# 768 features of the experts' second weights copied into 3 KB rows and gathered for the second 128 tokens, with the feature groups taken in turn

## The reference, cut to what matters

```
u = jnp.take(peer_u, expert, axis=0)
act = jax.nn.gelu(jnp.einsum('chkd,cd->chk', u, zc))
v = jnp.take(peer_v, expert, axis=0)
w = (gate * act.astype(jnp.float32)).astype(zc.dtype)
return jnp.einsum('chk,chkd->cd', w, v).astype(zc.dtype)
```

## Time and profile before

| | before |
|---|---|
| median of 3 runs | 3041.22 us |
| lowest, highest run | 3038.93, 3041.25 us |
| span of the profiled execution | 3039.3 us |
| TensorE busy | 3026.3 us of the span |
| VectorE, ScalarE, GpSimd busy | 2088.4, 1564.2, 1106.6 us |
| DMA, mean over the span | 221 GB/s |
| read and written | 627.88 MB, 39.99 MB |

### The profile page before, as it was taken

The page is one execution under the profiler, slowest core; times in us unless marked ns, Lnnn a source line. Parts: engine busy times, 40 slices in busy tenths (PEclk is TensorE's granted clock), DMA queues, the critical chain, the costliest instruction groups (busy, mean ns, idle before and its releaser), DMA issues.

```text
span 3039.3 us, 42704 instructions
## 1 busy us (share of the span) xinstructions
PE 3026.3 (100%) x16292; PEld 2605.3 (86%) x16292; DVE 2088.4 (69%) x3053; ACT 1564.2 (51%) x2160; POOL 1106.6 (36%) x856
## 2 busy tenths in 40 slices
PE   9999999999999999999999999999999999999999
PEld 7888888888888888888888888888888888888887
DVE  8957986555655656666667699998766856545554
ACT  7654554544544544444445656666566534444443
POOL 0023368888876377787771300000422000000000
PEclk9999999999999999999999999999999999999999
DMA  7567877988888899999997655555565566666664
GB/s 257 169 206 261 321 210 198 242 213 215 214 214 278 287 283 286 284 286 288 291 287 203 193 183 173 174 179 187 188 193 175 188 170 210 189 206 194 193 193 148
DMA packets 398365, 670.73 MB, mean 221 GB/s; under 512 B 68048, under 2 KB 293584, under 8 KB 394960
## 3 DMA queue, kind: packets, MB, share of 16 engines
q1 hardware_dynamic: 306144, 574.70, 61.2%
q10 hardware_dynamic: 42864, 76.28, 7.2%
q0 software_dynamic: 49152, 17.01, 4.5%
HBM read 627.88 MB, written 39.99 MB: 220 GB/s over the span
## 4 chain that ended last, share of the span: by engine, by line
PE 92%; DVE 3%; issue 2%; ACT 1%; DMA 1%; POOL 1%; SPq 0%; ACTq 0%; POOLq 0%; DVEq 0%
PE G L571 40%; PE G L575 20%; PE G L628 3%; PE G L626 3%; PE G L627 3%; PE M L626 3%; PE M L627 3%; PE M L628 3%; PE M L653 2%; PE G L653 2%; PE M L654 2%; PE G L655 2%; PE G L654 2%; PE M L655 2%; DVE lo L1364 1%
## 5 line engine op out<-in xcount | busy, mean ns | idle before, releaser
L571 PE MATMUL G<-ZA,hi 128*128 128x512 f32 x5098 | 1765.2, 395 | 4.4 <-DVE lo L1364 2.3
L1364 DVE TENSOR_TENSOR lo<-raw,hi 128x1024 fp32r<-128x1024 f32 x1088 | 1336.8, 1242 | 568.2 <-ACT hi L953 565.6
L953 ACT ACTIVATE hi<-raw 128x1024 fp32r<-128x1024 f32 x1088 | 1130.1, 1055 | 620.8 <-DMA raw<-in_pv 334.4
L575 PE MATMUL G<-ZA,lo 128*128 128x256 f32 x5114 | 1389.2, 278 | 0.0
L571 PEld LDWEIGHTS G<-ZA,hi 128*128 128x128 f32 x5098 | 943.2, 188 | 210.8 <-DVE lo L1364 2.8
L575 PEld LDWEIGHTS G<-ZA,lo 128*128 128x128 f32 x5114 | 960.7, 188 | 16.6
L2075 POOL DMA_INDIRECT g_scratch<-sel,IDX x256 | 418.6, 1635 | 112.9 <-issue 81.4
L960 ACT ACTIVATE tA<-G 128x256 f32<-128x256 f32 x367 | 139.4, 380 | 549.0 <-PE G L575 546.0
L1370 DVE TENSOR_TENSOR tS<-G,tA 128x256 f32<-128x256 f32 x336 | 141.2, 421 | 310.1 <-ACT tA L960 307.0
L2092 POOL DMA_INDIRECT vrow<-in_pv,IXV x192 | 259.2, 1350 | 109.3 <-issue 51.2
L626 PE MATMUL G<-hi,ZB 128*128 128x512 f32 x512 | 199.4, 389 | 0.0
(11 more groups left out here) (374 smaller groups left out, 2860.8 us busy)
## 6 DMA issues: line engine op xcount, KB each, us to landing
raw<-in_pu SPq DMA_DIRECT2D x256, 512.0 KB, 4.5
raw<-in_pv SPq DMA_DIRECT2D x256, 512.0 KB, 6.1
raw<-in_w_in SPq DMA_DIRECT2D x192, 512.0 KB, 3.5
raw<-in_w_up SPq DMA_DIRECT2D x128, 512.0 KB, 4.2
raw<-in_w_down SPq DMA_DIRECT2D x128, 512.0 KB, 5.0
raw<-in_w_out SPq DMA_DIRECT2D x32, 512.0 KB, 3.5
raw<-in_wq SPq DMA_DIRECT2D x32, 512.0 KB, 5.1
g_scratch<-zero ACTq DMA_DIRECT2D x16, 1024.0 KB, 6.9
```

The costliest lines, as they stand in the source:

```text
L571: pe.matmul(G[:, 0:512], w, Z[:, k, :], start=first, stop=False, skip_group_check=True)
L575: m = pe.matmul(G[:, 0:256], lo[POS[u][p] % NRAW][:, k % 8, :], weights(u, p)[1][:, k, 0:256], start=False, stop=last, skip_group_check=True)
L953: act.activation(hi[w][:, :, :], raw[r][:, :].rearrange("p (k n) -> p k n", k=8), ACT.Copy).then_inc(s_hi, 1)
L1364: dve.tensor_tensor(lo[r][:, :, :], raw[r][:, :].rearrange("p (k n) -> p k n", k=8), hi[w][:, :, :].bitcast(F32), ALU.subtract).then_inc(s ...
```

## The change

The stage v works with 768 gathered features instead of 256, for the second 128 tokens, and the rows come from a copy in DRAM.

- 96 DMAs on ScalarE's queue (`widen`) copy the last 768 features of all experts from `peer_v` into `v_wide`, DRAM to DRAM, 512 KB each, in pieces of 512 bytes that land 3 KB apart. 30 are issued in units 4 to 39, 66 in units 66 to 163.
- Each pick is then one indirect DMA of a 3 KB row for each of 128 tokens. The early pieces, their spill and their return go. GpSimd issues 128 gathers and 128 reads of activations, at 5/2 a unit, in blocks of 2 picks with a ring of 5 blocks.
- Matmuls of the second token half: group 2 has 256 columns instead of 512, group 3 has none instead of 256.
- In chunks 0 to 6 the units go through the four feature groups in turn (`expert_part`); the last chunk keeps its order. Loads and splits of gates are spread over the chunk to fit.
- `vacc` is three times as long as before and lies over the ring of `tS` and `tA`.
- `g_scratch` and `h_scratch` are laid out with one contiguous row of 33 x 1024 elements (132 KB) per partition.

```diff
-WIDE = 256
+WIDE = 768
+FROM_Q = 16 - WIDE // 128
-BLOCK = 8
+BLOCK = 2
-RING = 3
+RING = 5
+COPY_AT = {u: n for n, u in enumerate([u for u in range(4, 40) if u % 6] + list(range(66, 165, 3)) + list(range(67, 166, 3)))}
+PITCH = 33 * 1024
+def expert_part(i, c):
+    return divmod(i, 4) if c == KEPT - 1 else divmod(i, 4)[::-1]
+def last_use(c, n):
+    return VB[c] + (12 + n // 2 if c == KEPT - 1 else 4 * (n // 2) + 3), n % 2
 def gate_kept_at(u):
-    c, n = divmod(u - VB[0] + 10, 16)
-    return (c, n - 2) if 0 <= c < KEPT and n in range(2, 6) else None
+    if VB[0] - 8 <= u < VB[0] - 4:
+        return 0, u - VB[0] + 8
+    c, n = divmod(u - VB[0] - 2, 16)
+    return (c + 1, n // 4) if n % 4 == 0 and 0 <= c < KEPT - 1 else None
 def picks_by(u):
-    return max(0, min((FETCHED + BLOCK) * PIECES, (u - VB[0] + 1) * 3 // 1))
+    return max(0, min(2 * 128, (u - VB[0] + 1) * 5 // 2))
 DOTS_AT = {}
 for _b in range(PIECES):
-    _u = min(v for v in range(VB[0], F0) if picks_by(v) >= (FETCHED + BLOCK) * (_b + 1)) + 6
...
+    _u = min(v for v in range(VB[0], F0) if picks_by(v) >= 2 * BLOCK * (_b + 1)) + 4
+    DOTS_AT.setdefault(_u, []).extend(range(BLOCK * _b, BLOCK * _b + BLOCK))
                 for x in range(2):
                     for h, G in enumerate(VM[q]):
+                        e = min(512, max(0, 128 * (FROM_Q - 4 * q))) if h else 512
+                        if not e:
+                            continue
-                        e = EDGE if q == 3 and h else 512
-                        act.wait_ge(s_mm, done(VB[c] - 4 + n // 2, n % 2))
+                        act.wait_ge(s_mm, done(*last_use(c - 1, n)))
+            def widen(n):
+                q, a = divmod(n, 16)
+                src = ins["pv"][FROM_Q + q, a].rearrange("p (b f) -> (p b) f", f=128)
+                act.dma_start(vwide[1024 * a:1024 * a + 1024, 128 * q:128 * q + 128], src).then_inc(s_vw, 16)
                 if u == F0:
                     expert_out(3)
+                    act.wait_ge(s_ved, 4)
-                b, k = divmod(n, FETCHED + BLOCK)
-                if k < FETCHED:
+                b, k = divmod(n, 2 * BLOCK)
+                if k < BLOCK:
+                    if n == 0:
+                        pool.wait_ge(s_mm, done(VB[0] - 1))
+                        pool.wait_ge(s_ixa, 11)
+                        pool.wait_ge(s_vw, 16 * len(COPY_AT))
                     if k == 0:
+                        pool.wait_ge(s_vrow, ROW_BASE + 16 * BLOCK * b)
                         if b >= RING:
                             pool.wait_ge(s_dot, BLOCK * (b - RING + 1))
                     at = BLOCK * b + k
+                    pool.indirect_dma_start(vrow[:, slot_of(b), k, :], None, vwide,
+                                            bass.IndirectOffsetOnAxis(IXV[:, at:at + 1], 0)).then_inc(s_vrow, 16)
```

More of the change, by code:

```diff
@@ L213, in gates_split_at @@
         return 0, range(4, 8)
-    c, n = divmod(u - VB[0] + 3, 16)
-    return (c, (2 * n, 2 * n + 1)) if n < 4 and 0 < c < KEPT else None
+    c, n = divmod(u - VB[0] - 4, 16)
+    return (c + 1, (n // 2, n // 2 + 1)) if n % 4 == 0 and 0 <= c < KEPT - 1 else None
 def up_split_at(u):
@@ L302, in build @@
                      ("neg", [128, 384], F32)],
-                    [("zb_pad3", [128, 6144], F32), ("parts", [128, 3, T], F32)],
-                    [("stage", [128, EARLY * PIECES, 128], F32)])
+                    [("zb_pad3", [128, 6144], F32), ("parts", [128, 3, T], F32)])
         ry = region(16384, "y_mem",
@@ L339, in build @@
         IXV, IXA, gsp, asp = r1["IXV"], r1["IXA"], r3["gsp"], r3["asp"]
-        vrow, vacc, stage = za["vrow"], za["vacc"], zb["stage"]
+        vrow = za["vrow"]
         acc, tQ = [sb(f"acc{i}", [128, T]) for i in range(2)], [sb(f"tQ{i}", [128, T]) for i in range(2)]
         tcol = sb("tcol", [128, 2])
-        tA = [sb(f"tA{i}", [128, T]) for i in range(3)]
-        tS = [sb(f"tS{i}", [128, T]) for i in range(4)]
+        ts = region(7168, "ts_mem", [(f"tS{i}", [128, T], F32) for i in range(4)] + [(f"tA{i}", [128, T], F32) for i in range(3)],
+                    [("vacc", [128, 2, WIDE], F32)])
+        tA = [ts[f"tA{i}"] for i in range(3)]
+        tS, vacc = [ts[f"tS{i}"] for i in range(4)], ts["vacc"]
         GB = [ps(f"G{i}") for i in range(4)]
         MB = [ps(f"M{i}") for i in range(4)]
[L347 to L351, removed]
+        scr = nc.dram_tensor("g_scratch", [128 * PITCH, 1], F32, kind="Internal").ap()
+        gscr = scr.rearrange("(p f) o -> p (f o)", p=128)
+        hflat = nc.dram_tensor("h_scratch", [128 * PITCH, 1], F32, kind="Internal").ap()
+        hscr = hflat.rearrange("(p f) o -> p (f o)", p=128)
+        vwide = nc.dram_tensor("v_wide", [16384, WIDE], F32, kind="Internal").ap()
         row = nc.dram_tensor("row_scratch", [16, 128], F32, kind="Internal").ap()
@@ L1141, in clear_g @@
                 act.wait_ge(s_pad, 6)
[L1142 to L1158, removed]
+                act.dma_start(gscr[:, 2048 * n:2048 * n + 2048], zero[:, :]).then_inc(s_gz, 16)
+                if n == 15:
+                    for s in (gscr, hscr):
+                        act.dma_start(s[:, 128 * T:PITCH], zero[:, 0:PITCH - 128 * T]).then_inc(s_gz, 16)
+            def widen(n):
+                q, a = divmod(n, 16)
+                src = ins["pv"][FROM_Q + q, a].rearrange("p (b f) -> (p b) f", f=128)
+                act.dma_start(vwide[1024 * a:1024 * a + 1024, 128 * q:128 * q + 128], src).then_inc(s_vw, 16)
             def load_g(c, n):
-                size, k = 4 * 128 * T, slice(4 * n, 4 * n + 4)
-                at = size * (4 * c + n)
+                k, at = slice(4 * n, 4 * n + 4), T * (16 * c + 4 * n)
                 if c:
@@ L1297, in scalar_program @@
                         act.activation(sel[:, t, :], sel[:, t, :], ACT.Exp).then_inc(s_sfe, 1)
[L1298 to L1301, removed]
+                if u in COPY_AT:
+                    widen(COPY_AT[u])
                 if u == VB[0] - 16:
@@ L1304, in scalar_program @@
                     act.wait_ge(s_ind[1], 2048)
[L1305 to L1309, removed]
+                if load_g_at(u):
+                    load_g(*load_g_at(u))
+                if load_h_at(u):
+                    load_h(*load_h_at(u))
                 if u == F0 + 2:
@@ L1751, in expert_out @@
             def expert_out(q):
-                dve.wait_ge(s_mm, done(V_LAST + 4 * q + 3))
-                if q < 3:
-                    dve.tensor_copy(by_token(q, 1), VM[q][1][:, :]).then_inc(s_ved, 1)
-                else:
+                e = min(512, max(0, 128 * (FROM_Q - 4 * q)))
+                if e:
+                    dve.wait_ge(s_mm, done(V_LAST + 4 * q + 3))
+                    m = dve.tensor_copy(by_token(q, 1)[:, 0:e], VM[q][1][:, 0:e])
+                if e < 512:
+                    at = slice(512 * q + e - 128 * FROM_Q, 512 * q + 512 - 128 * FROM_Q)
                     dve.wait_ge(s_dot, 128)
-                    dve.tensor_copy(by_token(q, 1)[:, 0:EDGE], VM[q][1][:, 0:EDGE])
-                    dve.tensor_tensor(by_token(q, 1)[:, EDGE:512], vacc[:, 0, :], vacc[:, 1, :], ALU.add).then_inc(s_ved, 1)
+                    m = dve.tensor_tensor(by_token(q, 1)[:, e:512], vacc[:, 0, at], vacc[:, 1, at], ALU.add)
+                m.then_inc(s_ved, 1)
             def expert_add(n):
@@ L2160, in pool_program @@
                         scatter(t, h)
-                for n in range(early_by(u - 1), early_by(u)):
-                    if n == early_by(u - 1):
-                        pool.wait_ge(s_mm, done(u - 1))
-                    early_pick(n)
                 for n in range(picks_by(u - 1), picks_by(u)):
```

123 lines of the change are left out of this document (46 added, 77 removed).

## The result

| | before | after |
|---|---|---|
| median | 3040.74 us | 3094.81 us |
| lowest, highest of 4 runs | 3038.93, 3041.25 | 3085.24, 3102.58 |
| span of the profiled execution | 3039.3 us | 3100.8 us |

After stands to before as 1.0177 (95% interval 1.0160 to 1.0194): 54 us slower, where 15 us faster was forecast. It lies above the range.

The account below looks back on a forecast made before the run. TensorE was taken as the bound, with the DMA engines right under it in stage v. Terms of -20 (stage v), +3, +1 and +1 summed to -15 us, from 3041.2 to 3026 us; range 2975 to 3080.

Parts of the forecast that it names:

- The bound of before: Whole kernel before: TensorE bounds it, busy 3026.3 us of a span of 3039.3.
- TensorE's gain: Stage v: fewer columns in groups 2 and 3 take 87 us from TensorE, of which 67 go to waiting.
- the forecast's edge: End of stage v: the transposes there take 6 us.
- The bound of the DMA engines: Stage v's first 102 units: moving 184.6 MB takes 520 us, between 469 and 607.
- The landing of a gather: Stage v, GpSimd: a landing of 7.0 us makes a block 8.4 us and the pick part 520 us.
- The rival of the landing wait: GpSimd before each block: landing sets the pace, decides from 8.6 us a block; at 9.1, 3070 us; chance 0.21.
- the sign that I had named for this rival: Stage v: GpSimd idle for landings while the DMA share is under 1 would show the landing wait.
- the pick part: The first 102 units of stage v, in which the picks run, forecast to last 520 us.
- The copies: DRAM to DRAM copies: +3 us in stage u (0 to +27), +1 for the 30 early ones (0 to 5).
- The rival on the copies: Stage u: copies fill it at twice the price, +27 us instead of +3, 3050 us; chance 0.10.
- The page's other rule, queues served in turn: An engine takes packets of its queues in turn, so 1 KB weight packets get the smaller part while gathers run.
- The end of the stage: Stage v's last four group 3 units, 2.72 us each with 1 MB of weights each: 0 to 5 us, taken as 1.

Follow-up runs that it names:

- two counters: The changed kernel with landings counted on two semaphores in turn, so a block waits for the block before the last: 3017.01 us, ratio 0.9908.
- slower picks: The changed kernel with two counters and indirect DMAs at 9/4 a unit instead of 5/2, 768 features: 3003.81 us, ratio 0.9883.

## Why the prediction was wrong, point by point

**The bound of before, and TensorE's gain: right.** The starts in the new groups are as forecast where the clock is at its upper level (0.11 to 0.12 us apart with 256 columns, at 1103 us of after). In the kernel of 512 features, where group 3 has no second token half and nothing but TensorE binds, 128 units at 5.45 and 2.72 us make 19.07 x 32 = 610 us, and with the 6 us of the forecast's edge 616; measured 616.0 (1055.6 to 1671.6).

**The bound of the DMA engines: right, as the second bound.** The forecast had 51, 46 and 43 engine-us a MB for weights, gathers and loads, a share of 1.06, and 520 us. The kernel with two counters meets it. Its queues of 1060 to 1580 us (packets, MB, share):

```profile
q1 hardware_dynamic: 110583, 109.83, 66.9%
q0 software_dynamic: 14258, 50.00, 25.6%
q10 hardware_dynamic: 7343, 26.35, 13.3%
```

66.9% of 520 x 16 engine-us over 109.83 MB is 51 a MB, gathers 43, loads 42, at 359 GB/s. By the count of its matmuls the first 102 units end at 1560, 506 us after the start. Stage v takes 634 us there (1054.4 to 1688.5), where 641 was forecast for the whole.

**The landing of a gather: this step failed.** The prediction took 7.0 us from the start of a block's second gather to the next block, a block of 8.4, "the same as the DMA bound by chance". Measured: 7.7 us of landing and 0.6 us until the next gather starts, a term that the sum had at nothing, so a block of 9.7. The bounds, 6.1 and 8.7, held for the mean (8.3 with the 0.6). The choice between them was wrong: I built the lower end out of bytes (0.33 MB more at 394 GB/s adds 0.8 us to pieces of 64 KB), and stayed near it, though the fullest stretch of before had shown landings of 8.7 us for weights. Counted in the same way in every trace, the last of a block's gathers lands after 5.7 us in stage v of before (64 KB a gather, share 0.94), 6.1 with rows of 1 KB (128 KB, 0.92) and 7.7 in after (384 KB, 0.95): 2.0 us more from 64 to 384 KB where the forecast had 0.8. A fuller DMA doesn't explain the difference, since 384 KB take 7.3 us with two counters and 7.4 with slower picks, at a share of 1.06. An estimate that fits is that both gathers of a block must pass before it has landed: from 1 KB to 3 KB rows that is 0.52 MB, at the 311 GB/s of after 1.7 us, against the 1.6 measured. No run tests it, with one gather a block for instance.

The rival of the landing wait had place, price and turning point: past 8.6 us a block the change loses. Its formula, 64 x 9.6 - 18 + 121 = 717 us, gives the 717.6 that stage v took. The split within it is less good: by their matmuls the first 102 units end at 1638 (582 us, not 596), and the last 26 take 136 us instead of 115 and the edge, since the last gathers go out at 1667.9 only, beside units past the 102nd. I had priced the rival at 9.1 us a block and closed the range just above, at 3080; one at 9.6 is 717 - 661 + 5 = 61 us slower, 3102, which is the span's own +61.5. And the sign that I had named for this rival is what the trace shows: GpSimd idle for landings at a DMA share under 1. Two prices that come out equal at guessed middles are no support for each other: each should have stood in the range with its own far end (628 us for the pick part, which the text left out with less than 1 in 10).

**The wait's cover.** Before, a block's wait for gathers lay behind 12 gathers and 8 reads, a block of 8 picks; with blocks of 2 picks it lies behind the second gather itself and two reads, some 5 us by the lengths of the earlier trace rows, against a landing of 7.7. The change therefore turned a latency that stage v of before hides into the stage's pace. All that GpSimd waits there, in 1056 to 1590 us, for pieces to land in `vrow` is this:

```profile
POOL asp L2102 <- DMA vrow<-in_pv,IXV: 0.3, 1, 0.3
```
Two counters give the cover back: a block may be in flight while the next is issued, at no other cost.

**The copies: right, at the cheap end.** +3 and +1 were forecast, +1.4 measured in after's trace at the end of stage u and 1.4 in the run of the copies alone. Their price is within the bounds of 49 to 98: the writing queue goes from 8.3% for 14.82 MB to 29.8% for 48.90 MB in after,

```profile
q1 hardware_dynamic: 28567, 103.98, 55.9%
q10 hardware_dynamic: 80016, 48.90, 29.8%
```

so 34.1 MB cost 0.215 x 552 x 16 = 1899 engine-us, 56 a MB. Room came from the weights, whose share falls from 61.9% to 55.9% for the same bytes. By the rule of the Trainium skill that the prediction named (page "DMA: Bandwidth & Descriptors", section "Latency and other measured facts": 207 GB/s per direction between HBM tensors) these copies would have been an estimated 77 engine-us a MB; the traces do not agree, and the measurement decides. The page's row is for tiles with 16 KiB a partition at a row pitch of 512 KiB, which these copies don't have (pieces of 512 bytes, rows of 3 KB), so it is another case more than a wrong figure. The rival on the copies needed twice 49 engine-us a MB and fell with the measured 56. The page's other rule, queues served in turn, is not tested by any run here.

**The end of the stage: mis-sized.** I gave 1 us to the last light units, for the loads of their weights. Once the light group 3 ends the stage, TensorE waits for the expert output's additions on VectorE; in the version of 640 features, of 1640 to 1810 us:

```profile
PE M L712 <- DVE A L1765: 4.2, 1, 4.2
PE G L712 <- DVE A L1765: 3.2, 1, 3.2
```

7.4 us, where before had three waits of 1.0 us and less. After has three such waits, of 3.9, 2.5 and 1.2. What follows the last matmul of stage v is 1323.8 us in before (1715.5 to 3039.3), 1327.1 in after (1773.7 to 3100.8), and 1329.2 in the version of 640 features: +3 to +5 for the term of 1.

**What stays open.** The view of the waits gives 40 us of GpSimd's idle time before gathers to TensorE, 102 to a landing and 63 to nothing that it shows. By the counter's increments the part that isn't landing is small: beyond the 0.26 us that lie at least between the last increment and the next gather, all 63 blocks together lose 20 us, and TensorE coming back slowly after a gap (next section) can be no more than that in the pace of the blocks. Why a landing grows by 2.0 us from 64 to 384 KB was not tested by itself. The share of TensorE's lost clock in the time of the stage isn't separated either.

## What to carry to other kernels

Before a wait for a DMA is made shorter in its block (fewer transfers between issue and wait), take the time from issue to landing from the fullest stretch of the trace and leave room above it for a larger transfer (here 2.0 us more for 384 KB than for 64 KB, where the bytes at the highest rate gave 0.8), and set it against the work that the issuing engine has in between; where the work is shorter, alternate two counters so that one block is in flight while the next is issued. When work moves from a full engine to a nearly full one, choose its amount so that both are full: here 640 of 2048 features for half the tokens gave 2989.86 us, where 768 gave 3017, or 3004 at the same pace of picks, and 512 gave 3002. And where two bounds come out equal, keep the far end of each in the range.

## What the runs showed of the hardware

TensorE's granted clock falls after gaps in its work. In before it is 1.00 throughout stage v; in after it is 0.93 over 1060 to 1650 us. The timeline of TensorE behind a gap of 5.27 us in after (start us, us, instruction, idle time before it):

```profile
1305.39 0.79 PE L645 MATMUL G<-hi,ZB 128*128 128x512 f32 x1 [5.27 <-DVE lo L1369]
...
1307.90 0.63 PE L646 MATMUL G<-lo,ZB 128*128 128x512 f32 x1
1308.32 0.63 PE L647 MATMUL G<-hi,ZB 128*128 128x512 f32 x1
...
1310.82 0.40 PE L646 MATMUL M<-lo,ZB 128*128 128x512 f32 x1
1311.05 0.40 PE L647 MATMUL M<-hi,ZB 128*128 128x512 f32 x1
```

Starts are 0.42 us apart at 1308, the 1.2 GHz level, and 0.23 at 1311, the 2.4 GHz level; some 5 us run at the lower level and cost about 2.5 us more than they would at the upper one. So a gap of 5 us costs TensorE 7.5 there; in the version of 512 features, with no gaps, the clock is 1.00.

Small indirect DMAs land not much earlier than large ones here. From the start of a block's last gather of 128 rows to the last increment of its counter it takes 5.7 us with rows of 512 bytes (before), 6.1 with 1 KB and 7.7 with 3 KB (after), at DMA shares of 0.94, 0.92 and 0.95; with 3 KB rows at a share of 1.06 it takes 7.3 and 7.4. An indirect read of 128 single float32 took 6.72 and 7.34 us in two chain pieces of after, where the median was 5.2 before.

VectorE's multiply-add of 768 features takes 1017 ns by its record, and the starts of two in a row are 0.93 us apart, as the prediction had taken from the nearest width.
